# Two-block decoder kernel: the channel sums of the modulation written as rows, with a one-column selector, and turned once a stage

## What is computed

```python
c_act = jax.nn.silu(c)
ada = c_act @ w_ada[l] + b_ada[l]            # 1024 -> 3072 in block 1, 1024 -> 6144 in block 2
shift, scale, gate = jnp.split(ada, 3, axis=-1)
h = rmsnorm(x, norm_g[l]) * (1.0 + scale[:, None, :]) + shift[:, None, :]
...
x = x + gate[:, None, :] * y
```

## Time and profile before

| what | value |
|---|---|
| median of the runs | 2083.98 us |
| span of the profiled execution | 2082.3 us |
| TensorE busy | 2043.9 us, 98% |
| VectorE busy | 1752.0 us, 84% |
| ScalarE busy | 1321.4 us, 63% |
| granted TensorE clock, mean | 0.996 |

### The profile page before, as it was taken

The page is one execution under the profiler, slowest core; times in us unless marked ns, Lnnn a source line. Parts: engine busy times, 40 slices in busy tenths (PEclk is TensorE's granted clock), DMA queues, the critical chain, the costliest instruction groups (busy, mean ns, idle before and its releaser), DMA issues.

```text
span 2082.3 us, 33418 instructions
## 1 busy us (share of the span) xinstructions
PE 2043.9 (98%) x13361; PEld 1827.3 (88%) x13361; DVE 1752.0 (84%) x2155; ACT 1321.4 (63%) x1267; POOL 32.3 (2%) x60
## 2 busy tenths in 40 slices
PE   7999999999999999999999999999999999999998
PEld 5999999999999799999888888888888888888886
DVE  4998976888759778888769889898988989899897
ACT  4655645666645654435667777776777777777774
POOL 3000000000000000000000000000000000000000
PEclk9999999999999999999999999999999999999999
DMA  9887855766656479986548999999999999999995
GB/s 302 277 258 241 251 194 163 233 218 210 210 185 218 148 233 310 318 311 223 165 165 320 365 349 361 378 361 351 361 361 369 359 348 368 370 367 355 355 361 185
DMA packets 358817, 597.37 MB, mean 287 GB/s; under 512 B 10985, under 2 KB 204025, under 8 KB 358665
## 3 DMA queue, kind: packets, MB, share of 16 engines
q1 hardware_dynamic: 355072, 588.65, 81.9%
q0 software_dynamic: 2752, 5.86, 1.1%
q10 hardware_dynamic: 840, 0.73, 0.1%
HBM read 591.80 MB, written 4.22 MB: 286 GB/s over the span
## 4 chain that ended last, share of the span: by engine, by line
PE 83%; DVE 10%; ACT 3%; issue 2%; DMA 1%; POOL 0%; ACTq 0%; DVEq 0%; SPq 0%; POOLq 0%
PE ps L1755 10%; PE ps L1757 10%; PE ps L1756 10%; PE ps L1786 5%; PE ps L1785 5%; PE ps L1784 5%; PE ps L1192 5%; PE ps L1194 5%; PE ps L1193 5%; PE ps L1278 3%; PE ps L1279 3%; PE ps L1280 3%; DVE wlo L1853 3%; DVE qacc L2135 2%; DVE acc L1909 1%
## 5 line engine op out<-in xcount | busy, mean ns | idle before, releaser
L1853 DVE TENSOR_TENSOR wlo<-raw,whi 128x2048 fp32r<-128x2048 f32 x485 | 1108.9, 2289 | 187.6 <-ACT whi L772 184.9
L772 ACT CAST whi<-raw 128x2048 fp32r<-128x2048 f32 x485 | 926.6, 1911 | 337.4 <-PE ps L1757 123.5
L1192 PE MATMUL ps<-hhi,whi 128*128 128x256 f32 x1344 | 384.7, 286 | 0.0
L1193 PE MATMUL ps<-hlo,whi 128*128 128x256 f32 x1344 | 377.1, 281 | 0.0
L1194 PE MATMUL ps<-hhi,wlo 128*128 128x256 f32 x1344 | 376.9, 280 | 0.0
L1755 PE MATMUL ps<-whi,xghi 128*128 128x512 f32 x896 | 355.6, 397 | 0.8 <-DVE wlo L1853 0.8
L1757 PE MATMUL ps<-wlo,xghi 128*128 128x512 f32 x896 | 350.1, 391 | 0.0
L1756 PE MATMUL ps<-whi,xglo 128*128 128x512 f32 x896 | 349.4, 390 | 0.0
L1192 PEld LDWEIGHTS ps<-hhi,whi 128*128 128x128 f32 x1344 | 254.5, 189 | 3.8 <-issue 3.6
L1193 PEld LDWEIGHTS ps<-hlo,whi 128*128 128x128 f32 x1344 | 254.7, 190 | 0.2
L1194 PEld LDWEIGHTS ps<-hhi,wlo 128*128 128x128 f32 x1344 | 254.3, 189 | 0.0
(11 more groups left out here) (421 smaller groups left out, 2999.2 us busy)
## 6 DMA issues: line engine op xcount, KB each, us to landing
raw<-in_moe_w_gate_dram SPq DMA_DIRECT2D x112, 1024.0 KB, 6.0
raw<-in_moe_w_up_dram SPq DMA_DIRECT2D x112, 1024.0 KB, 6.2
raw<-in_moe_w_down_dram SPq DMA_DIRECT2D x112, 1024.0 KB, 5.3
raw<-in_w_in_dram SPq DMA_DIRECT2D x92, 1024.0 KB, 5.4
raw<-in_w_ada_dram SPq DMA_DIRECT2D x69, 1024.0 KB, 7.7
raw<-in_w_out_dram SPq DMA_DIRECT2D x24, 1024.0 KB, 5.3
raw<-in_ffn_w_gate_dram SPq DMA_DIRECT2D x11, 1024.0 KB, 8.8
raw<-in_ffn_w_up_dram SPq DMA_DIRECT2D x11, 1024.0 KB, 8.3
```

Of the source, the lines that this page charges most:

```text
L772: nc.scalar.copy(whi[:, u.hl, :], raw[:, u.raw, :]).then_inc(hi_ready, 1)
L1192: mm(ps2[u.bank][:, j], whi[:, u.hl, w], hhi[:, k], start=k == 0, stop=False)
L1193: mm(ps2[u.bank][:, j], whi[:, u.hl, w], hlo[:, k], start=False, stop=False)
L1853: V.tensor_tensor(wlo[:, u.hl, :], raw[:, u.raw, :], whi[:, u.hl, :].bitcast(F32), ALU.subtract).then_inc(raw_free, 1)
```

## The change

TensorE's part of a modulation unit is turned round. The weights are now 32 columns of a small table `place`, 128 x 64 numbers of zeros with a single column of ones, put into the tail of the tile `h`. The window is moved so that the ones stand at column `row`, the number of the unit in its stage. What moves past is `acc`, 128 columns at a time. So the sums over the partitions come out as row `row` of a 32 x 128 block: the first half of the unit in partitions 0 to 31, the second in 32 to 63 (`ROW_GROUPS = 2`). Units of a stage add up in the same block of `ps[7]`, each into its own row (the other rows get zeros). Once a stage VectorE copies the 64 x 128 block (`copy_sums`), TensorE turns it with one product with the identity (`turn_sums`), and VectorE takes the columns (`take_layer`, `take_mod`). `take_pair` at the third head is gone. `place_clear` writes the table anew with two memsets after the norm of each of the three stages, as `h` is written by the norms.

```diff
+        place = h[:, KD - 1, S - 2 * GROUP:S]
+        arows = acc[0:ROW_GROUPS * GROUP, 0, 0:ROW_COLS]
...
-            def ada(a, bank):
+            def ada(a, row, rows):
                 pe.wait_ge(ada_free, a.sums())
-                for j in range(2):
-                    last = mm(bank[:, a.col + j:a.col + j + 1], acc[:, a.n % HALF, j * P:(j + 1) * P], ones[:, 0:1],
-                              start=True, stop=True)
+                for g in range(ROW_GROUPS):
+                    last = mm(ps[7][GROUP * g:GROUP * g + GROUP, S:S + ROW_COLS], place[:, GROUP - 1 - row:2 * GROUP - 1 - row],
+                              acc[:, a.n % HALF, ROW_COLS * g:ROW_COLS * g + ROW_COLS], start=row == 0, stop=row == rows - 1,
+                              skip_group_check=True)
                 last.then_inc(ada_done, 1)
+            def turn_sums(stage, rows):
+                pe.wait_ge(row_copied, START_PAIRS + stage + 1)
+                of = ident[0:ROW_GROUPS * GROUP, 0:ROW_GROUPS * GROUP].rearrange("p (j i) -> p j i", j=2)
+                mm(ps[7][:, S + P:S + P + 2 * rows].rearrange("p (j i) -> p j i", j=2), arows, of[:, :, 0:rows], start=True, stop=True)\
+                    .then_inc(mod_turned, 1)
...
-                            if i == 0 and l + pair:
-                                pe.wait_ge(mod_taken, pair + (0, 2)[l])
+                            if l and i == pair == 0:
+                                pe.wait_ge(mod_taken, 1)
...
+                    if j == 2:
+                        turn_sums(l, NPAIR * ADA_TURN[l])
...
-                rows_product(Unit(S_FF + FF_UNITS + j), fhi, flo, 2 * j, j == 0, j == DOWN_UNITS - 1)
+                rows_product(Unit(S_FF + FF_UNITS + j), fhi, flo, 2 * j, j == 0, j == DOWN_UNITS - 1,
+                             (lambda: turn_sums(L, ADA_FF)) if j == DOWN_UNITS - 1 else None)
...
+            def place_clear(n):
+                dve.wait_ge(hlo_ready, KD * (norm_no(n) + 1))
+                step(V.memset(place, 0.0))
+                step(V.memset(place[:, GROUP - 1:GROUP], 1.0))
+            def copy_sums(last):
+                dve.wait_ge(ada_done, last)
+                V.tensor_copy(arows, ps[7][0:ROW_GROUPS * GROUP, S:S + ROW_COLS]).then_inc(row_copied, 1)
...
-                    if h_no == 2:
-                        take_pair(l, 0)
...
                     if j == 0:
-                        take_pair(l, 1)
-                    if j == 0:
+                        copy_sums((A_L1, A_MIX0)[l])
                         add_squares(Head(l, H - 1), 1)
                     if j == 2:
                         retention_finish(Head(l, H - 1))
+                    if j == 3:
+                        take_layer(l)
...
+                    place_clear(N_FFN[0])
...
-            dve.wait_ge(ada_done, A_MIX1)
-            take_mod(ps[7], 0, 4, *ADA_AT_FF[0][1:])
-            take_mod(ps[7], 8, ADA_FF - 4, *ADA_AT_FF[4][1:]).then_inc(mod_taken, 1)
+            copy_sums(A_MIX1)
+            dve.wait_ge(mod_turned, START_PAIRS + L + 1)
+            take_mod(0, ADA_FF, 4, *ADA_AT_FF[0][1:])
+            take_mod(4, ADA_FF, ADA_FF - 4, *ADA_AT_FF[4][1:]).then_inc(mod_taken, 1)
```

More of the change, by code:

```diff
@@ L63 @@
 RAW = 6
+ROW_GROUPS = 2
+ROW_COLS = 256 // ROW_GROUPS
+START_PAIRS = 4
 HALF = 3
@@ L180, in __init__ @@
     def __init__(self, n, first):
-        self.n, self.col = n, 2 * (n - first)
+        self.n, self.first = n, first
     def count(self, k=1):
@@ L1267, in token_products, with rows_product @@
                 last.then_inc(unit_done, 1)
-            def rows_product(u, hi, lo, tile, first, final):
+            def rows_product(u, hi, lo, tile, first, final, between=None):
                 pe.wait_ge(raw_free, u.free())
@@ L1282, in rows_product @@
                         last.then_inc(rows_done, 1)
+                    if between and i == 1 and d == 0:
+                        between()
                 last.then_inc(unit_done, 1)
@@ L1416, in ada_after @@
                         for i in ada_at(ADA_SUMMED[l][pair], h_no % 2 * HEAD_UNITS + j):
-                            if i == 0 and l + pair:
-                                pe.wait_ge(mod_taken, pair + (0, 2)[l])
-                            ada(ada_units[i][0], ps[7])
+                            if l and i == pair == 0:
+                                pe.wait_ge(mod_taken, 1)
+                            ada(ada_units[i][0], pair * ADA_TURN[l] + i, NPAIR * ADA_TURN[l])
                     if h_no:
@@ L1912, in ada, with take_mod @@
                 V.tensor_tensor(sums[0], sums[0], sums[1], ALU.add).then_inc(ada_free, 1)
-            def take_mod(bank, col, n, block, l, at):
+            def place_clear(n):
[5 more added lines that the diff above has]
+                V.tensor_copy(arows, ps[7][0:ROW_GROUPS * GROUP, S:S + ROW_COLS]).then_inc(row_copied, 1)
+            def take_mod(row, rows, n, block, l, at):
                 par, base = (par1, P1_BADA) if block == 0 else (par2, P2_BADA)
                 to = 3 * KD * (3 * l + block)
-                return V.tensor_tensor(mod[:, bass.ds(at * 2 + to, 2 * n)], bank[:, col:col + 2 * n],
-                                       par[:, l, bass.ds(at * 2 + base, 2 * n)], ALU.add)
+                sums = ps[7][:, S + P:S + P + 2 * rows].rearrange("p (j i) -> p j i", j=2)
+                return V.tensor_tensor(mod[:, at * 2 + to:at * 2 + to + 2 * n].rearrange("p (u j) -> p j u", j=2), sums[:, :, row:row + n],
+                                       par[:, l, at * 2 + base:at * 2 + base + 2 * n].rearrange("p (u j) -> p j u", j=2), ALU.add)
             def amuls(norms):
@@ L1979, in _ @@
             low(Unit(S_B1 + 1))
+            place_clear(0)
             gates_low(0)
@@ L2061, in retention_finish, with take_layer @@
                 y_low(hd, 1, KD)
-            def take_pair(l, pair):
-                ada_units = (ada_l0, ada_l1)[l](pair)
-                dve.wait_ge(ada_done, ada_units[-1][0].count())
+            def take_layer(l):
+                rows = NPAIR * ADA_TURN[l]
+                dve.wait_ge(mod_turned, START_PAIRS + l + 1)
                 if l == 0:
-                    take_mod(ps[7], 0, 2, *ada_units[0][1:])
-                    take_mod(ps[7], 4, 6, *ada_units[2][1:])
-                    take_mod(ps[7], 16, 1, *ada_units[8][1:]).then_inc(mod_taken, 1)
-                else:
-                    take_mod(ps[7], 0, ADA_TURN[1], *ada_units[0][1:]).then_inc(mod_taken, 1)
+                    for pair in range(NPAIR):
+                        first, units = pair * ADA_TURN[0], ada_l0(pair)
+                        take_mod(first, rows, 2, *units[0][1:])
+                        take_mod(first + 2, rows, 6, *units[2][1:])
+                        last = take_mod(first + 8, rows, 1, *units[8][1:])
+                else:
+                    last = take_mod(0, rows, rows, *ada_l1(0)[0][1:])
+                last.then_inc(mod_taken, 1)
             def angles():
@@ L2100, in _ @@
                     low(Unit(S_B1 + l * UNIT_L1 + 1))
+                    place_clear(l)
                     gates_low(l)
@@ L2197, in _ @@
                         retention_finish(Head(l, H - 1))
-                dve.wait_ge(mod_taken, (2, 4)[l])
+                    if j == 3:
+                        take_layer(l)
+                dve.wait_ge(mod_taken, l + 1)
                 if l == 0:
@@ L2384, in mixer @@
                 last.then_inc(mod_taken, 1)
-                dve.wait_ge(mod_taken, (5, 7)[l])
+                dve.wait_ge(mod_taken, (3, 5)[l])
                 amuls((N_FFN[l],))
```

6 lines of the change are left out of this document (3 added, 3 removed).

## The result

| kernel | median of the runs | lowest to highest | ratio to before, 95% interval |
|---|---|---|---|
| before | 2083.22 us (18 runs) | 2080.93 to 2086.72 | 1 |
| changed | 2087.18 us (18 runs) | 2084.85 to 2089.18 | 1.0017 [1.0011, 1.0023] |

The changed kernel is slower, by 3.5 us with 2.3 to 4.8 as the bounds (by the ratio and its interval; the quotient of the two medians alone is 1.0019, 4.0 us). The forecast had the sign and the cost of a unit right; its 5.3 us lie a little above the interval.

A forecast was written before the change was run, and what follows sets the result against it. TensorE, busy 98% of the span, was taken as the bound, so queue time is paid unless a wait covers it. Units 3.5, turns 1.5 and memsets 0.25 make 5.3 us more: 2089.3 us, range 2086.2 to 2092.5.

The forecast's parts named there:

- The unit: One modulation unit on TensorE, matmul ahead to second behind: 0.78 us against 0.69 before, 0.09 us more.
- rival of groups out of step: In each unit the second group starts only with the second half of the first: 2093.5 us, chance 0.09.
- Where it is paid: Modulation units where TensorE waits for nothing: 39 of 54 pay 0.09 us each, 3.5 us in all.
- the 23: Units of the feed-forward stage said to pay the 0.09 us; its first unit stands behind a 1.6 us wait.
- the nine: Nine units from 72 to 163.8 us, where VectorE sets the pace: said to cost nothing.
- the 16 in the heads: Units in the later heads, where TensorE waits for nothing: said to pay 0.09 us each.
- The turns: Three 64-row products on TensorE, in the out projections and ending the feed-forward stage: 0.50 us each, 1.5 us in all.
- The memsets: Two VectorE memsets ahead of the first sum of the feed-forward stage: 0.25 us; free at the start and in layer 1.
- The sum: Whole kernel: 3.5 + 1.5 + 0.25 = 5.3 us slower, 2089.3 us.
- one stretch fewer: TensorE's clock falls to half for one 3.4 us stretch less, behind waits near 162 or 769 us: 2087.9 us, chance 0.22.
- Faster, if widths change for free: Narrow weights next to full-width ones cost no pause: each unit 0.11 us shorter, 2080.7 us, chance 0.09.

The follow-up runs named there:

- amplified pair: One idle full-width matmul between the two halves of every modulation unit, in the changed kernel and the kernel before: 2134.85 us (ratio 1.0245) and 2100.31 us (1.0081).
- grouped_before: The kernel before with its modulation units summed in twos and threes, as in the grouped version of the changed kernel: 2083.00 us, ratio 0.9997.

## Why the prediction was right

- **The unit, 0.78 forecast, 0.77 measured,** piece by piece: in 0.21 and 0.21, between starts 0.14 and 0.14, out 0.20 and 0.20, follower 0.23 and 0.22. The rows that carried it were of other shapes (four groups of 32, two of 64). One of them decided: the earlier trace rows, which says that groups go in step. The rival of groups out of step is refuted at every unit.
- **Where it is paid, 39 of 54.** The amplified pair gives 16 and 23. At the real price the 23 and the nine hold, and of the 16 in the heads 12 to 14 show, 0.2 to 0.3 us less than counted.
- **The turns, 0.50 forecast, 0.53 measured,** all three without a wait.
- **The memsets, 0.25 forecast, 0.3 measured** from the wait for the first sum, 1.9 against 1.6 us; they take 0.17 us themselves.
- **The sum, 5.3 forecast, 3.5 [2.3, 4.8] measured.** The pieces at their measured sizes give 39 x 0.087 + 3 x 0.53 + 0.3 = 5.3, so it is not a piece that was mis-sized. What did not hold is the step that let all of it reach the end and counted the half-clock stretches as fixed. The prediction gave "one stretch fewer" a chance of 0.22 and the time 2087.9. That rival is what the profiled run shows, and its second trace has two fewer. But the median, 2087.18, lies near 2087.9 for another reason, by chance: the timed runs of the changed kernel have only 0.3 of a stretch less, some 0.5 us, and at an equal listed clock they are still 2.9 to 3.8 us slower and not 5.3. The heads account for another 0.3 us. About 1 us, less than the interval is wide, stays open. A taker is seen in two traces: an execution that comes early to the feed-forward stage waits there for sums, and the kernel before, being the faster one, would lose more by it. That this happens in its timed runs was not shown; its one trace without idle matmuls has no such wait. A small slip beside it: the runs lie 1.9 us above their own spans, not 1.7.
- **Faster, if widths change for free.** Refuted by the 0.21 in and 0.20 out at every unit, and by the 0.12 in where one width is kept.

## What to carry to other kernels

On an engine that is busy 98% of the time, price a small matmul from the matmul ahead to the second one behind, at the widths of its neighbours: here narrow weights saved 0.11 us between a unit's own starts, and the changes of width took 0.09 on each side. If narrow weights are wanted, put several of such products into one visit (three units cost 0.40 us each, one alone 0.77), but ask then for sums that are ready, or the wait takes the saving back. A difference of 0.2% is read more surely from the same matmul's start at both ends of a stage, or from a version that multiplies the disputed cost, than from medians alone. A version that multiplies a cost also outgrows its cover, so a count of places made with it holds for its own price. And before a missing microsecond is put down to the clock, compare runs that list the same clock.

## What was not expected of the hardware

- A start of accumulation in one half of a bank reaches sums that are still being added up in the other half. With an idle matmul of 256 columns started anew in `ps[7]` the output was off by a relative 1.3, though it wrote to other columns; started without that, the output was whole. That it was the eight rows summed by then that were lost is read from the order of the program, not from the sums themselves. In the kernel before, where each unit's columns are finished at once, the same start beside eight finished units left the output whole.
- The stretches of 3.4 us at 1.2 GHz behind waits of 1.0 to 1.9 us come in some executions of a program and not in others: at 770 us in the first trace of the changed kernel (18 instructions) and not in the second (31). The one near 165 us stands in both traces of old units without idle matmuls (`before`, `grouped_before`) and in none of the four of new units without them, which is suggestive and no more.
- A half-clock stretch takes 1.5 us where it stands, but runs of one kernel whose listed clock is lower by one stretch are only some 0.5 us longer.
- Two fp32 matmuls of 128 columns to two column groups take no longer than one: 0.34 us from the first start to the next product in both.
